# Sixty-four experts: where TensorE turns the gated values of the expert before

## What is computed

```python
scores = jax.nn.sigmoid(x2d @ w_router)            # choose 8 of 64 experts for each token
...
def swiglu(x, w_gu, w_down):
    g, u = jnp.split(x @ w_gu, 2, axis=-1)         # w_gu 1024 x 512, w_down 256 x 1024
    return (jax.nn.silu(g) * u) @ w_down
...
out = lax.map(expert_block, (buf_tok, block_e))    # each expert on its own tokens
routed = zeros.at[buf_tok].add(out * buf_w)        # weighted sum over the 8 experts of a token
```

## Time and profile before

| what | us |
|---|---|
| median of three runs | 1967.46 (1962.0 to 1968.35) |
| the profiled execution | 1963.43 |
| its span, first to last instruction | 1961.3 |
| TensorE busy | 1864.2 (95%) |
| VectorE busy | 956.7 (49%) |
| ScalarE busy | 523.4 (27%) |
| GpSimd busy | 334.5 (17%) |
| first gate and up product of expert 0 | 596.8 |
| last down products end | about 1215.5 |

### The profile page before, as it was taken

How to read it: one execution, slowest core, us unless ns; L and a number is a source line. 1 busy time by engine, 2 the same in 40 slices (tenths; PEclk the granted TensorE clock), 3 DMA queues, 4 the chain that set the end, 5 groups by cost and what they waited for, 6 DMA issues and landing times. The chain is left out here.

```text
span 1961.3 us, 28010 instructions
## 1 busy us (share of the span) xinstructions
PE 1864.2 (95%) x10606; PEld 1038.3 (53%) x10606; DVE 956.7 (49%) x2029; ACT 523.4 (27%) x1154; POOL 334.5 (17%) x297
## 2 busy tenths in 40 slices
PE   8999899999998999999999998999999999999997
PEld 3334348854443344444444333457756688888443
DVE  5987748623474233233223325623375554454643
ACT  2448731200211333333333332320264100000000
POOL 0655430000037101001000114400023000000000
PEclk9999999999999999999999999999999999999998
DMA  6114042212356999999999999622310122222411
GB/s 251 64 49 121 22 149 86 86 43 110 151 193 216 377 404 405 400 404 404 406 407 405 399 402 372 233 90 98 129 44 2 43 108 86 86 86 86 138 55 43
DMA packets 80480, 375.40 MB, mean 191 GB/s; under 512 B 13458, under 2 KB 13714, under 8 KB 55184
## 3 DMA queue, kind: packets, MB, share of 16 engines
q1 hardware_dynamic: 55728, 303.59, 40.4%
q10 hardware_dynamic: 11824, 37.02, 5.3%
q0 software_dynamic: 12848, 33.74, 4.7%
HBM read 352.64 MB, written 33.07 MB: 197 GB/s over the span
## 5 line engine op out<-in xcount | busy, mean ns | idle before, releaser
L2843 DVE COPY slab<-bank 32x512 f32<-32x512 f32 x124 | 80.8, 688 | 393.9 <-PE bank L1491 393.9
L1090 PE MATMUL bank<-ring,slab 128*128 128x512 f32 (+1 forms) x608 | 254.3, 578 | 3.6 <-DMA ring<-stream 2.6
L1483 PE MATMUL bank<-slab 128*32 128x512 f32 x1536 | 230.1, 601 | 16.2 <-DVE slab L2799 6.0
L1483 PE MATMUL bank<-ring,slab 128*32 128x512 f32 x1536 | 227.0, 595 | 14.0 <-DVE slab L2799 4.5
L1491 PE MATMUL bank<-ring,slab 128*32 128x512 f32 x512 | 229.6, 602 | 0.0
L1491 PE MATMUL bank<-slab 128*32 128x512 f32 x480 | 212.5, 596 | 0.0
L1090 PEld LDWEIGHTS bank<-ring,slab 128*128 128x128 f32 x608 | 115.9, 192 | 136.4 <-issue 132.0
L3255 POOL TENSOR_TENSOR small<-small 128x1 f32<-128x1 f32 (+2 forms) x30 | 27.5, 921 | 825.3 <-DVE small L2308 825.3
L1090 PE MATMUL bank<-slab,ring 128*128 128x512 f32 (+1 forms) x368 | 148.2, 559 | 2.6 <-ACT slab L1845 1.8
L1483 PEld LDWEIGHTS bank<-slab 128*32 128x32 f32 x1536 | 72.2, 111 | 147.2 <-issue 141.5
L1483 PEld LDWEIGHTS bank<-ring,slab 128*32 128x32 f32 x1536 | 71.2, 110 | 143.8 <-issue 140.6
(11 more groups left out here) (363 smaller groups left out, 3030.8 us busy)
## 6 DMA issues: line engine op xcount, KB each, us to landing
ring<-stream SPq DMA_DIRECT2D x173, 512.0 KB, 4.4
slab<-w_exp_gu SPq DMA_DIRECT2D x64, 1024.0 KB, 14.0
ring<-w_exp_gu SPq DMA_DIRECT2D x64, 1024.0 KB, 13.6
ring<-w_exp_down SPq DMA_DIRECT2D x32, 1024.0 KB, 22.0
slab<-w_exp_down SPq DMA_DIRECT2D x32, 1024.0 KB, 22.6
y_rows<-slab ACTq DMA_DIRECT2D x64, 384.0 KB, 8.2
y_rows<-zeros ACTq DMA_DIRECT2D x1, 3456.0 KB, 20.5
gb<-rows ACTq DMA_DIRECT2D x5, 512.0 KB, 4.5
```

The lines of the kernel that those rows point to most:

```text
L1090: mm = nc.tensor.matmul(dst, lhs[k], rhs[k], start=(k == 0), stop=(k == len(lhs) - 1))
L1483: mm = nc.tensor.matmul(g_bank[32 * g:32 * g + 32, :], x[:, k, 32 * g:32 * g + 32], w[:, 512 * k:512 * k + 512], start=(k == 0), stop=(k = ...
L2843: i = nc.vector.tensor_copy(ye[b % 2][32:64, 512 * half:512 * half + 512], bank[5 + half][96:128, :])
```

## The change

The two transposes of the gated values leave the head of the block. In block e the values of expert e-1 (not e-2) are turned between the slices k = 3 and k = 4. From block 1 on every block does it. VectorE's copies of the turned values move behind `hidden` and `y_rest` of the same block, and ahead of `combine` in the last one. Of the two turns behind the last block one remains. The wait for `ht_ready` e-1 ahead of the products stays.

```diff
-                if down:
-                    if b >= 3 or first > 0:
-                        pe.wait_ge(ht_ready, e - 2)
-                    turn_hidden(b % 2, hid_ready, e - 1, ht_full)
...
                 for k in range(KD):
                     if k > 0:
                         turn_next(k)
+                    if k == 4 and (b >= 1 or first > 0):
+                        turn_hidden((b + 1) % 2, hid_ready, e, ht_full)
                     for g in range(3):
...
-            pe.wait_ge(ht_ready, NE - 2)
-            turn_hidden(0, hid_ready, NE - 1, ht_full)
             pe.wait_ge(ht_ready, NE - 1)
             turn_hidden(1, hid_ready, NE, ht_full)
...
-                if b >= 2 or steady:
-                    hidden_turned(b % 2, ht_full, e - 1, ht_ready)
                 if b >= 1 or steady:
                     if b >= 3 or steady:
                         dve.wait_ge(ht_full, e - 2)
                     hidden((b + 1) % 2, silu_ready, e, hid_ready)
                 if b >= 3 or steady:
                     y_rest(e - 3, (b + 1) % 2)
+                if b >= 1 or steady:
+                    hidden_turned((b + 1) % 2, ht_full, e, ht_ready)
                 if slot_ is not None:
                     for t in range(NT):
                         combine(slot_, t)
...
-            hidden_turned(0, ht_full, NE - 1, ht_ready)
             hidden(1, silu_ready, NE, hid_ready)
```

## The result

The changed kernel takes 1976.66 us (median of five runs, 1972.22 to 1978.26) against 1967.46 before (five runs on record, with the median and the extremes given above): the ratio is 1.0047, 95% interval 1.0033 to 1.0060. Measured once more beside other kernels it took 1973.94 against 1966.96, 1.0033 (1.0020 to 1.0045). So by the medians it is 7 to 9 us slower. All ratios and intervals in this document are those on record; they are not the quotients of the two medians beside them, and differ from these by up to 0.0013. A ratio of 1.001 is 2 us. The profiled execution has a span of 1970.3 us, 9.0 more than before.

A forecast was written before the change was run, and what follows sets the result against it. The DMA engines' weight queue was taken to bound the expert stage, not TensorE. Loop 0, block 1 +2.1, block 63's start 0 and VectorE there +1.5 gave +3.6 us, forecast 1969.5, range 1961 to 1977.

The forecast's parts named there:

- the rival with 1974.4: Block 1's delay is not absorbed if the gathers of experts 4 and 5 slip equally: +8.5 us, 1974.4; chance 0.18.
- the loop: Steady blocks: TensorE's block falls from 9.29 to 8.96 us, but the DMA engines need 9.61; gain 0 at the end.
- the transitions of blocks 1 and 4: Two changes between row transposes and products seen without idle time; the basis for taking 0.05 us for the middle turn.
- my upper bound, 0.17: Most that the tiling change in the middle of the products could cost, if the two transposes overlap with nothing: 0.17 us.
- the lead: The weight queue's lead over TensorE in the loop, shrinking by 0.65 us a block rather than 0.32, lasting to about 870.
- the cover of 0.65 us: DMA time per loop block beyond TensorE's; a middle turn costing more than 0.7 us would begin to show.
- the length of the wait: In block 1 TensorE stands at k = 4 for VectorE's gated values of expert 0, 609.4 to about 613.75: 4.3 us.
- how much of this reaches the end: Block 1 ends 7 us later; later waits absorb most, and the full queue moves by 2.1 us, bounds 0 and 7.
- the chain: From block 1 through lists and gathers to block 4, which starts 1.7 to 2 us late.
- The list of expert 4: ScalarE asks for it at about 621 instead of 619.46; its gather follows at about 626 instead of 624.43.
- Released by weights: Block 63's start is set by the down weights of expert 61, landing at 1198.7; taking VectorE out gains 0.
- VectorE's order: In block 63 copies of turned values precede the weighted sums, delaying the last turn: +1.5 us, bounds 1.2 and 2.0.

The follow-up runs named there:

- the half-weight pair: Only half of each down weight loaded from expert 4 on: kernel before 1957.5 us, changed kernel with both repairs 1948.21, against 1969.94.
- before, with and without the wait: Kernel before, with one wait added: in block 1 TensorE waits ahead of slice 4 for expert 0's gated values; no transposes moved; 1969.85 us against 1966.62.
- block 1 turned late: Changed kernel, but in block 1 alone the turn goes back behind the products and row transposes; 1971.85 us against 1966.62 for the kernel before.
- sums ahead of copies: Changed kernel, but VectorE in block 63 does the four weighted sums before the copies of the turned values; 1976.4 us against 1966.62 before.
- both repairs: Changed kernel with block 1's turn late and block 63's weighted sums ahead of the copies of turned values; 1968.14 us against 1966.62 before.

## Why the prediction was right where it was, and where not

The range (1961 to 1977) held the two medians, 1976.66 only just. The likeliest value, 1969.5, was 4 to 7 us too low, and of the classes the one that I gave 0.72, no change to be told within 0.3%, did not come: at 0.33% and 0.47% the kernel is slower. The nearest forecast was the rival with 1974.4. The direction was right; that the time still lies in the range owes as much to the range's upper bound as to the sum.

**Right: the loop.** It is bound by the weight queue; its gain ended in waits for down weights at 404 to 398 GB/s, and the half-weight pair shows the 9.3 us that lie hidden behind it. The middle turn, though, costs 0.43 us and not 0.27: I took 0.05 for the change of tiling, near the transitions of blocks 1 and 4, and even my upper bound, 0.17, was under the 0.21 measured. Those transitions were rows of one change next to a wait or a stage's end, and I read "no idle time" as "no cost": a busy span hides it, the distance between starts shows it. So the lead lasted until block 36 (943 us) and not until 870, and a down weight asked for at 832 was under way for 21.7 us, not 26. It changed nothing at the end, as the cover of 0.65 us held. The Trainium skill states in TensorEngine Tiling (Array Packing), Key Properties, that a change of tiling mode drains TensorE. Here that was the better guide than my two transitions: the traces fit it, at 0.21 to 0.24 us for a change and back, though they do not show that the time is a drain.

**Right in kind, wrong in size: block 1.** The place, the cause and the length of the wait (4.3 forecast, 4.47) and the end of the block (620 forecast, row transposes at 621.2) came as said. The step that was mis-sized is "how much of this reaches the end", 2.1 us forecast. Three pairs of kernels differ in block 1 alone. At expert 63 they say 4.6 us (before, with and without the wait), 3.8 and 4.2 (the changed kernel's two traces against block 1 turned late) and 3.5 (sums ahead of copies against both repairs), each with the scatter of 3 us named above. In the time the first pair says 3.2 us (1.0 to 5.7), the second 2 to 5. So it is some 3 to 5 us where 2.1 was forecast. The whole difference of the changed kernel at expert 63, 7.0 to 7.3, is more than block 1; what the other 3 us are is open (below).

What was wrong in the chain can be read. I had block 4 start 1.7 to 2 us late; it started 4.4 late (645.77), 3.6 if the 0.8 of the later first product is taken off. Two terms. The list of expert 4 I let land in the 4.2 us it took before; asked for behind the 2 MB of weights that the late block 1 had just released, it took 6.5, and the gather went out at 629.46 and not near 626. (In the three kernels with both repairs or block 1's, as many weights and no stall, it took 7.7 to 8.5 but was asked for 4 to 5 us earlier than before; counted from the first product of expert 0 it landed 25.5 to 26.4 us in, against 26.8 before and 31.0 in the changed kernel.) And the chain did not end with block 4: the gather of expert 6 held block 5 for another 2.40 us, which before had its rows in time, and the clock fell again (block 5's products from 657.82 to 661.17 at the slow level). My rival "the stall passes whole" named the list and the weights in one queue's way, with 1974.4; I gave it 0.18 because the list had waited until 619.46 for another reason. Its condition, row transposes of block 1 that end later than about 623, was not met (they end at 622.07), and the chain slipped all the same: it is decided by what the list and the gathers meet on their way and not by that moment.

**Block 63.** Released by weights, as forecast: now the profile says so itself (0.96, DMA). VectorE's order: 1.5 us forecast; the last turn came 11.1 us behind block 63's first product instead of 9.4, so 1.7. And in three of four traces with the late sums the idle time of 2.74 us brought the slow clock with it, 1.3 to 1.7 us more (8.32 and 8.73 against 7.03). In the fourth, the changed kernel's second trace, the slow clock was in block 63 itself (9.2 us). The forecast had no clock here: from block 63's start to the shared expert it is 3.1 and 3.4 us more than before in the two traces, about twice the term.

**The sum.** 0 + 2.1 + 0 + 1.5 = 3.6 was forecast; by the traces it is 7.0 to 7.3 at expert 63 and 3.1 to 3.4 from there to the shared expert, 10.4 together; the medians say 7.0 and 9.2. Both terms were too small, 2.1 for 3 to 5 and 1.5 for 3.1 to 3.4, and some 3 us before expert 63 are in neither.

**What stays open.** Of the 6.2 to 6.7 us that block 1 delays expert 6, the kernel before with the wait had 4.6 left at expert 63, and its median rose by 3.2. So a part of the delay is made good in the loop and behind it, and how is not shown. The other way round, the kernels with the middle turn and no stall are at 602.2 to 605.2 at expert 63, 0.1 to 3.1 behind the one before. From expert 25's to expert 58's down weights landings are 9.65 to 9.66 us apart in five traces with the middle turn, 9.61 to 9.63 in three more, and 9.59 to 9.60 in the two with full weights that turn at the head. Over 33 landings that would be up to 2 us. Whether the turn in the middle spoils the transfers a little, or it is chance, one profile each does not tell.

## What to carry to other kernels

When a queue is full for hundreds of microseconds and the time from issue to landing grows, do not expect time from a shorter loop body: look for what decides when that queue first becomes full, and hold every new wait in the first rounds against it. Moving a step one round earlier in a pipeline takes a round of slack from all its producers; the loop had that slack, the first rounds and the last did not, since there the same engines still did the work before and after it. And the price of a change of tiling is read from the distance between the starts of the products around it, not from idle time.

## What the hardware showed that I had not expected

- Transposes set between 32-column products cost 0.21 to 0.24 us more than beside other transposes, with no idle time shown for it; I take this for the price of the change of tiling there and back.
- A small fetch landed in 1.6 us ahead of 2 MB of weights, in 6.5 behind them in the changed kernel, and in up to 8.5 behind them in the others; a gather of 96 rows in 4.3 and, behind the weights, 8.9.
- An idle time of TensorE of 2.74 us brought the clock down in some executions and not in others: the last down products behind it took 7.03, 8.32 and 8.73 us. The stretch at their start, in the changed kernel and in its second execution, with the granted clock third from the end (0.61 and 1.00):

```profile
1218.00:1222.00 4.00, 3.84 (x8) 1.64 (x9) 2.47 (x6) 0.00 (x0) 3.09 (x4) 0.61 0.86 290
```

```profile
1221.00:1225.00 4.00, 3.52 (x10) 1.53 (x11) 2.80 (x6) 0.00 (x0) 3.12 (x3) 1.00 0.81 295
```

- In the rest of the program, behind the first product of the shared expert, which no edit touches, profiled executions differ by up to 7 us.
